# TensorE's program for an expert with further passes: one interleaved stretch instead of a detour and back

## The chip, the cores and the metric

One core of one Trainium2 chip. The metric is the device time of one execution in microseconds (us).

## The reference, cut to what matters

A two-layer encoder over 256 tokens of 1024 channels, all float32. Each layer has a mixing part (three groups of heads side by side between two projections) and an expert part. The change touches the second alone:

```python
g_sel = argmax(g_logits)                      # one of 4 groups per token
top_p, top_i = top_k(softmax(e_logits of that group), 2)
weights = one_hot(expert_id, 32) * combine    # two experts per token
hg, hu = t @ w_gate[e], t @ w_up[e]           # 1024 -> 512, for each of 32 experts
out += (silu(hg) * hu * weights[:, e]) @ w_down[e]   # 512 -> 1024
```

Every expert has 6.3 MB of weights (gate, up and down of 2 MB each), and all 32 of each layer are read from HBM.

## The kernel before, in words

**Passes.** The kernel computes an expert only for tokens that chose it, 32 at a time (`SLOTS`). Each expert has one pass of its own; if more than 32 tokens chose it, further passes ("extra") come before the own one. How many is counted on the chip and read into registers (`extra_passes`, L422, and `passes_before`, L418). A pass is, on TensorE (PE):

- `gather` (L587): 8 matmuls pick the tokens into bank `b_prep`. Each float32 matmul of this kernel is two in the trace, with two weight loads, so the trace has 16.
- `places` (L595): two transposes put the weighted places into `b_places`.
- `hidden` (L601): 32 matmuls (64 in the trace) with gate and up into `b_gate`. It waits for both chunks to have landed.
- `down` (L627): 16 matmuls (32) into `b_y`.
- `combine` (L643): 8 matmuls (16) add the result to the sums in banks 0 to 3.

Between them, VectorE (DVE) compares ranks and weighs (`prep`, L1195), transposes and scales the tokens (`tokens_ready`, L1211), and, behind ScalarE's (ACT) tanh (`act_tanh`, L974), multiplies and transposes the activation (`activate`, L1200). ACT copies `b_places` (`places_copy`, L983) and `b_y` (`y_copy`, L979). The semaphores come in two sets, `M` for own passes and `V` for further ones; `th`, `actT` and the banks are shared by both, while `PwTx` and `ysbx` are the further passes' own copies.

**Order.** In an expert without a further pass, PE runs hidden, gather for the next expert, combine of the expert before, down, places for the next expert (L906 to L928). The code of the own passes lies one behind the other (`pe_expert_n`), and at its end each tests whether the next expert has further passes (L908). If it has, PE jumps to a block `pe_extra_n` behind all own passes of both layers (L941 to L963). There a loop runs gather, places, hidden, down and combine in that order, once for each further pass, and PE jumps back to `pe_expert_n`. Each such block's loop body is written out for its own expert.

**Weights.** They go through a ring of 11 chunks of 2 MB in SBUF during the expert part (`RING` 8 and `LATE` 3, L71). SyncE (SP) issues the loads in a fixed order, each behind the wait for the chunk that held its slot (`wait_freed`, L466): gate and up are free after the own pass's `hidden` (`M["hidden_mm"]`), down after its `down` (`M["down_mm"]`), L483. The experts 0 and 31 of a layer (`EDGES`) load gate and up in halves.

Of the kernel before, what the change touches and what calls it, by code (L numbers as in the profile page):

```python
# [6 lines left out]
ALU = mybir.AluOpType  # L7
ACT = mybir.ActivationFunctionType
# [50 lines left out]
NE = NG * EPG  # L59
FF = 512  # L60
FC = FF // P
SLOTS = 32
NQ = P // SLOTS
GQ, DQ = FF // NQ, D // NQ
MORE = SEQ // SLOTS - 1
HALF = KC // 2
# [179 lines left out]
def build_encoder(nc, x_in, cols, rows, w_in, w_out, w_router, w_gate, w_up, w_down, final_w, out):  # L246
    with ExitStack() as ctx:
# [117 lines left out]
        Pw = [sb(f"Pw{i}", [P, TT, P], at=q) for i in range(2)]  # L365
# [4 lines left out]
        Pb = [sb(f"Pb{i}", [P, TT, SLOTS], at=m2) for i in range(2)]  # L370


        PwT = [sb(f"PwT{i}", [P, TT, P], at=scratch) for i in range(2)]
        PwTx = sb("PwTx", [P, TT, P], at=scratch)
        xg = [sb(f"xg{i}", [P, KC, SLOTS], at=scratch) for i in range(2)]
        ysb = sb("ysb", [P, DQ], at=scratch)
        ysbx = sb("ysbx", [P, DQ], at=scratch)
# [44 lines left out]
        def extra_passes(eng, e):  # L422
            return eng.value_load(more[0:1, e:e + 1], min_val=0, max_val=MORE)
# [159 lines left out]
        def _(pe):  # L583
# [3 lines left out]
            def gather(S, picks):  # L587

                for t in range(TT):
                    for j in range(NQ):  # L590
                        last = mm(b_prep[j * SLOTS:(j + 1) * SLOTS, 0:DQ], picks[:, t, :], xh[:, t, j * DQ:(j + 1) * DQ],  # L591
                                  start=(t == 0), stop=(t == TT - 1))
                last.then_inc(S["gather_mm"], 1)

            def places(S, weighted):  # L595

                for t in range(TT):
                    last = tr(b_places[:, t * P:(t + 1) * P], weighted[:, t, :], ident[:, :])  # L598
                last.then_inc(S["places_mm"], 1)

            def hidden(S, tokens, li, e):  # L601

                if e in EDGES:
                    for half, part in enumerate(("front", "back")):
                        slot, signal, count = chunk(li, part, e)
                        both = ring[:, slot, :].rearrange("p (h n) -> p h n", h=2)
                        pe.wait_ge(signal, count)
                        for k in range(HALF):
                            for j in range(NQ):
                                o = k * FF + j * GQ  # L610
                                last = mm(b_gate[j * SLOTS:(j + 1) * SLOTS, 0:2 * GQ], tokens[:, half * HALF + k, :],  # L611
                                          both[:, :, o:o + GQ], start=(half + k == 0), stop=(half == 1 and k == HALF - 1))
                        last.then_inc(S["hidden_mm" if half else "front_mm"], 1)
                    return

                (a, a_signal, a_count), (b, b_signal, b_count) = chunk(li, "gate", e), chunk(li, "up", e)
                low, high = min(a, b), max(a, b)
                pe.wait_ge(a_signal, a_count)
                pe.wait_ge(b_signal, b_count)
                for k in range(KC):  # L620
                    for j in range(NQ):
                        o = k * FF + j * GQ
                        last = mm(b_gate[j * SLOTS:(j + 1) * SLOTS, 0:2 * GQ], tokens[:, k, :],  # L623
                                  ring[:, low:high + 1:high - low, o:o + GQ], start=(k == 0), stop=(k == KC - 1))
                last.then_inc(S["hidden_mm"], 1)

            def down(S, li, e):  # L627

                slot, signal, count = chunk(li, "down", e)
                if e == NE - 1:  # L630
                    pe.wait_ge(last_down_half, 16 * (li + 1))
                else:
                    pe.wait_ge(signal, count)
                for c in range(FC):
                    if e == NE - 1 and c == FC // 2:
                        pe.wait_ge(signal, count)
                    for j in range(NQ):
                        o = c * D + j * DQ
                        last = mm(b_y[j * SLOTS:(j + 1) * SLOTS, 0:DQ], actT[:, c * SLOTS:(c + 1) * SLOTS],  # L639
                                  ring[:, slot, o:o + DQ], start=(c == 0), stop=(c == FC - 1))  # L640
                last.then_inc(S["down_mm"], 1)

            def combine(S, places_, y):  # L643

                for t in range(TT):
                    for j in range(NQ):
                        r = slice(j * SLOTS, (j + 1) * SLOTS)
                        last = mm(ps[j][:, t * DQ:(t + 1) * DQ], places_[r, t, :], y[r, :],  # L648
                                  start=False, stop=False, skip_group_check=True)
                last.then_inc(S["combined"], 1)  # L650

            for li in range(DEPTH):
# [253 lines left out]
                for e in range(NE):  # L906
                    n = first + e + 1
                    pe.br_lt(extra_passes(pe, e), 1, on_true=f"pe_expert_{n}", on_false=f"pe_extra_{n}")  # L908
                    left_at[n] = nc.cur_bb
                    nc.switch_bb(f"pe_expert_{n}")  # L910
                    pe.wait_ge(M["xg_ready"], n)
                    hidden(M, xg[e % 2], li, e)
                    if e == 0:
                        pe.wait_ge(M["prep_ready"], 2 * first + 2)
                        places(M, Pw[0])
                    if e + 1 < NE:
                        pe.wait_ge(M["prep_ready"], 2 * n + 1)
                        gather(M, Pb[(e + 1) % 2])
                    if e > 0:
                        pe.wait_ge(M["y_copied"], n - 1)  # L920
                        pe.wait_ge(M["places_copied"], n - 1)
                        combine(M, PwT[(e - 1) % 2], ysb)
                    pe.wait_ge(M["actT_ready"], n)
                    down(M, li, e)
                    if e + 1 < NE:
                        pe.wait_ge(M["prep_ready"], 2 * n + 2)
                        pe.wait_ge(M["places_copied"], n)
                        places(M, Pw[(e + 1) % 2])  # L928
# [12 lines left out]
            for li in range(DEPTH):  # L941
                for e in range(NE):
                    n = li * NE + e + 1
                    nc.switch_bb(f"pe_extra_{n}", parent=left_at[n])
                    more_e = extra_passes(pe, e)
                    prev = passes_before(pe, e)
                    with pe.Fori(0, more_e) as j:
                        i = prev + j + 1
                        pe.wait_ge(V["prep_ready"], 2 * i)
                        gather(V, Pb[(e + 1) % 2])  # L950
                        if n > 1:
                            pe.wait_ge(M["places_copied"], n - 1 if e == 0 else n)
                        places(V, Pw[(e + 1) % 2])
                        pe.wait_ge(V["xg_ready"], i)
                        hidden(V, xg[(e + 1) % 2], li, e)
                        if n > 1:
                            pe.wait_ge(M["y_copied"], n - 1)
                        pe.wait_ge(V["actT_ready"], i)
                        down(V, li, e)
                        pe.wait_ge(V["places_copied"], i)  # L960
                        pe.wait_ge(V["y_copied"], i)
                        combine(V, PwTx, ysbx)
                    pe.br(f"pe_expert_{n}")  # L963
            nc.switch_bb("pe_experts_over", parent=last_at)


# [1 line left out]
        def _(act):  # L968
# [5 lines left out]
            def act_tanh(S, li, e, n):  # L974
                act.wait_ge(S["hidden_mm"], n)
                o = gate_half(li, e)
                A(th[:, :], b_gate[:, o:o + GQ], ACT.Tanh, scale=0.5).then_inc(S["tanh_ready"], 1)  # L977

            def y_copy(S, y, n):  # L979
                act.wait_ge(S["down_mm"], n)  # L980
# [159 lines left out]
        def _(dve):  # L1140
# [59 lines left out]
            def activate(S, li, e, n):  # L1200

                dve.wait_ge(S["tanh_ready"], n)
                o = gate_half(li, e)
                v.scalar_tensor_tensor(th[:, :], th[:, :], 1.0, b_gate[:, o:o + GQ], ALU.add, ALU.mult)  # L1204
                dve.drain()
                v.scalar_tensor_tensor(th[:, :], th[:, :], 0.5, b_gate[:, GQ - o:2 * GQ - o], ALU.mult, ALU.mult)
                dve.drain()
                v.transpose(actT[:, :].rearrange("p (c s) -> p c s", c=FC), th[:, :].rearrange("p (q c) -> p c q", c=FC)  # L1208
                            ).then_inc(S["actT_ready"], 1)
# [382 lines left out]
```

## Time and profile before

| | |
|---|---|
| median of 3 runs | 1186.97 us (1186.21 to 1187.02) |
| the profiled execution | 1185.0 us, of which the span is 1183.3 us |
| matmuls (PE), weight loads (PEld) busy | 923.9 us (78%), 587.3 us (50%) |
| DVE, ACT busy | 354.0 us (30%), 202.8 us (17%) |
| share of the DMA queue for data | 88.0% of 16 engines' span |
| HBM read | 433.20 MB |

The span runs from the first instruction to the last of the profiled execution; what is left to its time lies around it. The busy shares are averages over two mixing parts, in which the transfers mostly wait for slots, and two expert parts (about 150 to 590 us and 740 to 1170 us), in which most weights are read. "Issue" in a chain of waits is time in which an engine waited for nothing that the profile shows. A line number is that of the kernel before.

### The profile page before, as it was taken

Reading aid. Unit: us, or ns where it says so; the run is one execution under the profiler, and the core shown is the slowest. Engines: PE = TensorE matmul, PEld = TensorE weight load, DVE = VectorE, ACT = ScalarE, POOL = GpSimd, SP = SyncE. Lnnn points to the kernel's source line nnn. Section 1 sums busy time; section 2 is a strip of 40 time slices with the busy share of each in tenths; the row PEclk is TensorE's granted clock in tenths of the full one; section 3 lists DMA queues with packets and bytes.
Section 4 is the critical chain, followed back from the end, with each engine's and each line's share of the span. In section 5 each row is a group of like instructions: output and inputs, shape, how many; then the busy total and the mean of one; then the engine's idle time right before and its main releaser. Section 6 shows DMA issues by size and latency. Waiting matters only on the chain.

```text
span 1183.3 us, 26463 instructions
## 1 busy us (share of the span) xinstructions
PE 923.9 (78%) x11004; PEld 587.3 (50%) x11004; DVE 354.0 (30%) x1165; ACT 202.8 (17%) x600; POOL 8.1 (1%) x24
## 2 busy tenths in 40 slices
PE   7999889667678786986699988996666666765954
PEld 6877745333344443553388777453333333433532
DVE  4666343111112232231166645321111111111213
ACT  2275211000001010110124652110000000000001
POOL 2000000000000000000000000000000000000000
PEclk9999989887889998998899999898888888888977
DMA  9853489999999999999996326899999999999995
GB/s 340 319 223 143 151 337 428 429 429 430 429 428 428 429 429 428 412 427 431 405 399 257 124 99 252 353 429 428 430 431 427 431 430 428 431 429 428 428 427 208
DMA packets 50633, 436.17 MB, mean 369 GB/s; under 512 B 9408, under 2 KB 13760, under 8 KB 24640
## 3 DMA queue, kind: packets, MB, share of 16 engines
q1 hardware_dynamic: 50496, 434.26, 88.0%
q8 instruction: 96, 1.57, 0.5%
q14 instruction: 41, 0.34, 0.1%
HBM read 433.20 MB, written 1.05 MB: 367 GB/s over the span
## 4 chain that ended last, share of the span: by engine, by line
PE 46%; DMA 39%; DVE 4%; issue 4%; SPq 2%; DVEq 2%; ACT 1%; ACTq 0%
DMA ring<-in_w_up 38%; PE ps L623 13%; PE ps L711 8%; PE ps L639 5%; PE ps L855 5%; PE ps L648 3%; PE ps L591 3%; PE ps L727 2%; PE ps L611 2%; SPq L462 1%; PE ps L716 1%; DMA ring<-in_w_in 1%; SPq L464 1%; PE ps L824 1%; PE ps L774 1%
## 5 line engine op out<-in xcount | busy, mean ns | idle before, releaser
L623 PE MATMUL ps<-ring,xg 128*32 128x256 f32 x4352 | 314.2, 452 | 173.9 <-DMA ring<-in_w_up 168.6
L623 PEld LDWEIGHTS ps<-ring,xg 128*32 128x32 f32 x4352 | 170.0, 129 | 301.4 <-issue 239.9
L1204 DVE SCALAR_TENSOR_TENSOR th<-th,ps 128x128 f32<-128x128 f32 x72 | 20.7, 287 | 588.1 <-ACT th L977 588.1
L639 PE MATMUL ps<-ring,actT 128*32 128x256 f32 x2304 | 139.2, 382 | 14.1 <-issue 13.2
L977 ACT ACTIVATE th<-ps 128x128 f32<-128x128 f32 x72 | 20.0, 277 | 510.2 <-PE ps L623 474.2
L639 PEld LDWEIGHTS ps<-ring,actT 128*32 128x32 f32 x2304 | 69.0, 109 | 75.3 <-DVE actT L1208 22.6
L591 PE MATMUL ps<-xh,Pb 128*32 128x256 f32 x1152 | 79.5, 394 | 23.4 <-issue 19.4
L711 PE MATMUL ps<-hT,ring 128*128 128x256 f32 x416 | 93.5, 382 | 1.0 <-ACT hT L1014 0.8
L711 PEld LDWEIGHTS ps<-hT,ring 128*128 128x128 f32 x416 | 77.8, 190 | 15.0 <-issue 4.4
L648 PE MATMUL ps<-ysb,PwT 32*128 32x256 f32 x992 | 71.6, 403 | 0.0
L981 ACT ACTIVATE ysb<-ps 128x256 f32<-128x256 f32 x64 | 24.5, 383 | 223.9 <-PE ps L639 223.9
L591 PEld LDWEIGHTS ps<-xh,Pb 128*32 128x32 f32 x1152 | 38.8, 113 | 48.0 <-issue 23.5
L855 PE MATMUL ps<-ring,hT 128*128 128x256 f32 x256 | 59.2, 389 | 2.0 <-DVE hT L1426 2.0
L648 PEld LDWEIGHTS ps<-ysb,PwT 32*128 32x128 f32 x992 | 45.2, 186 | 27.5 <-issue 26.1
L855 PEld LDWEIGHTS ps<-ring,hT 128*128 128x128 f32 x256 | 49.0, 194 | 9.8 <-DVE hT L1426 2.4
L1214 DVE STREAM_TRANSPOSE xg<-ps 128x256 f32<-128x256 f32 x72 | 29.9, 415 | 37.3 <-PE ps L591 37.2
L1076 ACT ACTIVATE pbuf<-pbuf,low 128x256 f32<-128x256 f32 x56 | 28.0, 500 | 30.4 <-DVE low L1387 28.4
L1191 DVE TENSOR_TENSOR Pw<-Pb,W 128x256 f32<-128x256 f32 x72 | 30.6, 425 | 7.0 <-issue 0.5
L1216 DVE TENSOR_TENSOR xg<-xg,fnw 128x256 f32<-128x256 f32 x72 | 30.6, 425 | 5.8 <-issue 0.5
L598 PE MATMUL ps<-ident,Pw 128*128 128x128 f32 x144 | 32.3, 307 | 0.0
L1208 DVE STREAM_TRANSPOSE actT<-th 128x128 f32<-128x128 f32 x72 | 29.3, 407 | 6.2 <-issue 0.9
L598 PEld LDWEIGHTS ps<-ident,Pw 128*128 128x128 f32 x144 | 14.7, 143 | 30.8 <-DVE Pw L1191 16.1
(259 smaller groups left out, 681.5 us busy)
## 6 DMA issues: line engine op xcount, KB each, us to landing
ring<-in_w_down SPq DMA_DIRECT2D x62, 2048.0 KB, 40.4
ring<-in_w_gate SPq DMA_DIRECT2D x60, 2048.0 KB, 45.2
ring<-in_w_up SPq DMA_DIRECT2D x60, 2048.0 KB, 46.9
ring<-in_w_in SPq DMA_DIRECT2D x6, 2048.0 KB, 15.5
ring<-in_w_out SPq DMA_DIRECT2D x4, 2048.0 KB, 18.6
ring<-in_w_gate SPq DMA_DIRECT2D x8, 1024.0 KB, 29.3
ring<-in_w_up SPq DMA_DIRECT2D x8, 1024.0 KB, 31.3
ring<-in_w_in SPq DMA_DIRECT2D x6, 1024.0 KB, 16.0
```

Of the source, the lines that this page charges most:

```text
L591: last = mm(b_prep[j * SLOTS:(j + 1) * SLOTS, 0:DQ], picks[:, t, :], xh[:, t, j * DQ:(j + 1) * DQ], start=(t == 0), stop=(t == TT - 1))
L598: last = tr(b_places[:, t * P:(t + 1) * P], weighted[:, t, :], ident[:, :])
L623: last = mm(b_gate[j * SLOTS:(j + 1) * SLOTS, 0:2 * GQ], tokens[:, k, :], ring[:, low:high + 1:high - low, o:o + GQ], start=(k == 0), stop ...
L639: last = mm(b_y[j * SLOTS:(j + 1) * SLOTS, 0:DQ], actT[:, c * SLOTS:(c + 1) * SLOTS], ring[:, slot, o:o + DQ], start=(c == 0), stop=(c == ...
L648: last = mm(ps[j][:, t * DQ:(t + 1) * DQ], places_[r, t, :], y[r, :], start=False, stop=False, skip_group_check=True)
L711: last = mm(bank[:, 0:SEQ], lhs, hT[:, k, :], start=(k == 0), stop=(k == KC - 1))
L855: last = mm(bank[:, t * DQ:(t + 1) * DQ], mixT[:, c, t * P:(t + 1) * P], w_half[c // OUT_ROWS][:, c % OUT_ROWS, j * DQ:(j + 1) * DQ], star ...
L1076: last = A(pb[:, t, :], pb[:, t, :], ACT.Exp, bias=low[:, u, t:t + 1], scale=-1.0, accum_out=den[:, u, t:t + 1])
L1191: return v.tensor_tensor(weighted[:, :, :].rearrange("p t (j s) -> p t j s", j=NQ), picks[:, :, :].unsqueeze(2).broadcast_to(four), W[:, : ...
L1208: v.transpose(actT[:, :].rearrange("p (c s) -> p c s", c=FC), th[:, :].rearrange("p (q c) -> p c q", c=FC)).then_inc(S["actT_ready"], 1)
L1214: v.transpose(to[:, :, :], b_prep[:, 0:DQ].rearrange("p (q k) -> p k q", k=KC))
L1216: v.tensor_tensor(to[:, :, :], to[:, :, :], fnw[:, :].unsqueeze(2).broadcast_to([P, KC, SLOTS]), ALU.mult).then_inc(S["xg_ready"], 1)
```

## The change

An expert 2 to 30 of a layer that has a further pass gets a block in which the last further pass and the own pass are one stretch. PE first combines the expert before, then runs any further passes but the last in a loop as before, guarded by a test, and then, in this order: gather and places (further), hidden (further), hidden (own), down (further), gather for the next expert, combine (further), down (own), places for the next expert. Its last instruction jumps to the next expert's own block or further-pass block. The own block of that expert isn't run then.

The first product of a further pass goes to the bank `b_places` instead of `b_gate`, and ACT's tanh and DVE's activation read it there. So PE waits for ACT's copy of the places before that product and no longer before the combine. The order on ACT, DVE and SP is unchanged.

```diff
 def hidden(S, tokens, li, e):
+    to = b_places[:, 0:2 * GQ] if S is V else b_gate[:, 0:2 * GQ]
...
-                    last = mm(b_gate[j * SLOTS:(j + 1) * SLOTS, 0:2 * GQ], tokens[:, k, :],
+                    last = mm(to[j * SLOTS:(j + 1) * SLOTS, :], tokens[:, k, :],
...
                     pe.br_lt(extra_passes(pe, e), 1, on_true=f"pe_expert_{n}", on_false=f"pe_extra_{n}")
-                    left_at[n] = nc.cur_bb
-                    nc.switch_bb(f"pe_expert_{n}")
+                    left_at[n] = nc.cur_bb if e < 3 else left_at[n - 1]
+                    nc.switch_bb(f"pe_expert_{n}", parent=left_at[n])
...
                     nc.switch_bb(f"pe_extra_{n}", parent=left_at[n])
                     more_e = extra_passes(pe, e)
                     prev = passes_before(pe, e)
-                    with pe.Fori(0, more_e) as j:
-                        i = prev + j + 1
-                        pe.wait_ge(V["prep_ready"], 2 * i)
-                        gather(V, Pb[(e + 1) % 2])
-                        if n > 1:
-                            pe.wait_ge(M["places_copied"], n - 1 if e == 0 else n)
-                        places(V, Pw[(e + 1) % 2])
-                        pe.wait_ge(V["xg_ready"], i)
-                        hidden(V, xg[(e + 1) % 2], li, e)
-                        if n > 1:
-                            pe.wait_ge(M["y_copied"], n - 1)
-                        pe.wait_ge(V["actT_ready"], i)
-                        down(V, li, e)
-                        pe.wait_ge(V["places_copied"], i)
-                        pe.wait_ge(V["y_copied"], i)
-                        combine(V, PwTx, ysbx)
-                    pe.br(f"pe_expert_{n}")
+                    own = 2 <= e < NE - 1
+                    if own:
+                        pe.wait_ge(M["y_copied"], n - 1)
+                        pe.wait_ge(M["places_copied"], n - 1)
+                        combine(M, PwT[(e - 1) % 2], ysb)
+                    def whole(count):
+                        with pe.Fori(0, count) as j:
...
+                    if own:
+                        with pe.If(more_e > 1):
+                            whole(more_e - 1)
+                    else:
+                        whole(more_e)
+                    if not own:
+                        pe.br(f"pe_expert_{n}")
+                        continue
+
+                    i = prev + more_e
+                    pe.wait_ge(V["prep_ready"], 2 * i)
+                    gather(V, Pb[(e + 1) % 2])
+                    pe.wait_ge(M["places_copied"], n)
+                    places(V, Pw[(e + 1) % 2])
+                    pe.wait_ge(V["places_copied"], i)
+                    pe.wait_ge(V["xg_ready"], i)
+                    hidden(V, xg[(e + 1) % 2], li, e)
+                    pe.wait_ge(M["xg_ready"], n)
+                    hidden(M, xg[e % 2], li, e)
+                    pe.wait_ge(V["actT_ready"], i)
+                    down(V, li, e)
+                    pe.wait_ge(M["prep_ready"], 2 * n + 1)
+                    gather(M, Pb[(e + 1) % 2])
+                    pe.wait_ge(V["y_copied"], i)
+                    combine(V, PwTx, ysbx)
+                    pe.wait_ge(M["actT_ready"], n)
+                    down(M, li, e)
+                    pe.wait_ge(M["prep_ready"], 2 * n + 2)
+                    places(M, Pw[(e + 1) % 2])
+                    pe.br_lt(extra_passes(pe, e + 1), 1, on_true=f"pe_expert_{n + 1}", on_false=f"pe_extra_{n + 1}")
...
-                A(th[:, :], b_gate[:, o:o + GQ], ACT.Tanh, scale=0.5).then_inc(S["tanh_ready"], 1)
+                A(th[:, :], (b_places if S is V else b_gate)[:, o:o + GQ], ACT.Tanh, scale=0.5).then_inc(S["tanh_ready"], 1)
...
-                v.scalar_tensor_tensor(th[:, :], th[:, :], 1.0, b_gate[:, o:o + GQ], ALU.add, ALU.mult)
+                both = b_places[:, 0:2 * GQ] if S is V else b_gate[:, 0:2 * GQ]
+                v.scalar_tensor_tensor(th[:, :], th[:, :], 1.0, both[:, o:o + GQ], ALU.add, ALU.mult)
```

The body of `whole` is the loop body of before with the wait for `V["places_copied"]` moved ahead of `hidden`.

## Rows read from the trace of the kernel before

**Rows 1.** The page: its span, PE, transfer rate by slice, instruction queue.

```profile
span 1183.3 us, 26463 instructions
...
PE 923.9 (78%) x11004; PEld 587.3 (50%) x11004; DVE 354.0 (30%) x1165; ACT 202.8 (17%) x600; POOL 8.1 (1%) x24
...
GB/s 340 319 223 143 151 337 428 429 429 430 429 428 428 429 429 428 412 427 431 405 399 257 124 99 252 353 429 428 430 431 427 431 430 428 431 429 428 428 427 208
...
q8 instruction: 96, 1.57, 0.5%
```

**Rows 2.** The chain in order of time (start, us, what): two landings.

```profile
206.49 48.69 DMA ring<-in_w_up
...
264.50 49.19 DMA ring<-in_w_up
```

**Rows 3.** The same chain: an expert without a further pass.

```profile
441.17 0.86 PE ps L591 x16
442.03 1.08 PE ps L648 x16
443.11 1.86 PE ps L639 x32
444.97 0.37 PE ps L598 x2
```

**Rows 4.** ACT's copies of `b_y`: own ones to 323.5 us, all further ones.

```profile
L981 ACT ACTIVATE ysb<-ps x14: 383/383/384, 167.7 to 322.8; 128x256 f32<-128x256 f32 x14
...
L981 ACT ACTIVATE ysbx<-ps x8: 383/383/384, 340.4 to 1101.7; 128x256 f32<-128x256 f32 x8
```

**Rows 5.** SP's timeline (start, us, what): two loads with none between.

```profile
452.80 0.33 SPq L464 DMA_DIRECT2D ring<-in_w_up  x1
486.49 0.33 SPq L464 DMA_DIRECT2D ring<-in_w_down  x1
```

**Rows 6.** SP's line L464, time from issue to landing.

```profile
DMA to landing us min/median/max: 7.5/39.9/50.9
```

**Rows 7.** Windows (PE, PEld, DVE, ACT, POOL busy, then PEclk, DMA share, GB/s).

```profile
458.00:462.00 4.00, 2.56 (x18) 0.90 (x18) 0.61 (x2) 0.09 (x1) 0.00 (x0) 0.50 1.01 426
482.00:486.00 4.00, 4.00 (x76) 2.41 (x72) 0.00 (x0) 0.00 (x0) 0.00 (x0) 1.00 0.93 397
486.00:490.00 4.00, 4.00 (x72) 2.18 (x64) 2.39 (x7) 0.28 (x1) 0.00 (x0) 1.00 0.86 332
```

**Rows 8.** The chain again: expert 18 with one further pass.

```profile
370.66 3.64 PE ps L623 x64
...
379.16 1.11 PE ps L591 x16
...
381.30 3.66 PE ps L623 x64
384.96 1.60 issue
...
388.55 0.39 ACT ysbx L981
...
389.08 1.15 PE ps L648 x16
390.23 3.63 PE ps L623 x64
```

**Rows 9.** The chain again: stops at and in the further passes.

```profile
323.17 6.37 issue
329.54 1.97 PE ps L591 x16
...
357.76 0.93 issue
...
362.53 0.52 issue
...
453.14 6.17 issue
```

More of the change, by code:

```diff
@@ L610, in hidden @@
                                 o = k * FF + j * GQ
-                                last = mm(b_gate[j * SLOTS:(j + 1) * SLOTS, 0:2 * GQ], tokens[:, half * HALF + k, :],
+                                last = mm(to[j * SLOTS:(j + 1) * SLOTS, :], tokens[:, half * HALF + k, :],
                                           both[:, :, o:o + GQ], start=(half + k == 0), stop=(half == 1 and k == HALF - 1))
@@ L963, in _ @@
-                    pe.br(f"pe_expert_{n}")
+                    own = 2 <= e < NE - 1
[5 more added lines that the diff above has]
+                        with pe.Fori(0, count) as j:
+                            i = prev + j + 1
+                            pe.wait_ge(V["prep_ready"], 2 * i)
+                            gather(V, Pb[(e + 1) % 2])
+                            if n > 1:
+                                pe.wait_ge(M["places_copied"], n - 1 if e == 0 else n)
+                            places(V, Pw[(e + 1) % 2])
+                            pe.wait_ge(V["places_copied"], i)
+                            pe.wait_ge(V["xg_ready"], i)
+                            hidden(V, xg[(e + 1) % 2], li, e)
+                            if n > 1:
+                                pe.wait_ge(M["y_copied"], n - 1)
+                            pe.wait_ge(V["actT_ready"], i)
+                            down(V, li, e)
+                            pe.wait_ge(V["y_copied"], i)
+                            combine(V, PwTx, ysbx)
@@ new lines, in _ @@
+                    if own:
[7 more added lines that the diff above has]
+                    i = prev + more_e
+                    pe.wait_ge(V["prep_ready"], 2 * i)
+                    gather(V, Pb[(e + 1) % 2])
+                    pe.wait_ge(M["places_copied"], n)
@@ new lines, in _ @@
+                    places(V, Pw[(e + 1) % 2])
+                    pe.wait_ge(V["places_copied"], i)
+                    pe.wait_ge(V["xg_ready"], i)
+                    hidden(V, xg[(e + 1) % 2], li, e)
+                    pe.wait_ge(M["xg_ready"], n)
+                    hidden(M, xg[e % 2], li, e)
+                    pe.wait_ge(V["actT_ready"], i)
+                    down(V, li, e)
+                    pe.wait_ge(M["prep_ready"], 2 * n + 1)
+                    gather(M, Pb[(e + 1) % 2])
@@ L964, in _ @@
+                    pe.wait_ge(V["y_copied"], i)
+                    combine(V, PwTx, ysbx)
+                    pe.wait_ge(M["actT_ready"], n)
[3 more added lines that the diff above has]
+                    pe.br_lt(extra_passes(pe, e + 1), 1, on_true=f"pe_expert_{n + 1}", on_false=f"pe_extra_{n + 1}")
             nc.switch_bb("pe_experts_over", parent=last_at)
@@ L1203, in activate @@
                 o = gate_half(li, e)
-                v.scalar_tensor_tensor(th[:, :], th[:, :], 1.0, b_gate[:, o:o + GQ], ALU.add, ALU.mult)
+                both = b_places[:, 0:2 * GQ] if S is V else b_gate[:, 0:2 * GQ]
+                v.scalar_tensor_tensor(th[:, :], th[:, :], 1.0, both[:, o:o + GQ], ALU.add, ALU.mult)
                 dve.drain()
-                v.scalar_tensor_tensor(th[:, :], th[:, :], 0.5, b_gate[:, GQ - o:2 * GQ - o], ALU.mult, ALU.mult)
+                v.scalar_tensor_tensor(th[:, :], th[:, :], 0.5, both[:, GQ - o:2 * GQ - o], ALU.mult, ALU.mult)
                 dve.drain()
```

## The prediction

> **What bounds the kernel now.** I read the page first. PE is busy for 78% of the span, but the transfers run at 427 to 431 GB/s in nearly every slice of both expert phases [rows 1]: from the 7th slice of 29.6 us to the 19th, but for 412 in the 17th, and from the 27th to the 39th. Outside these phases they run at a third or two thirds of that, waiting for slots or for work. The shares of the page's chain don't say which of the two sets the length, so I went to single steps of the chain in order of time. In the expert phase one landing of an `up` chunk ends at 206.49 + 48.69 = 255.18 us and another, four experts later, at 264.50 + 49.19 = 313.69 us [rows 2]: 14.63 us an expert. An expert without a further pass costs PE 3.6 + 0.86 + 1.08 + 1.86 + 0.37 = 7.8 us [rows 3, 8]. So the transfers are the bound of both phases, and PE has slack wherever it isn't more than the depth of the ring behind them.
>
> The further passes are eight, and before the first of them 14 experts of layer 1 have copied their product [rows 4]. The timeline of these copies puts them at experts 15, 17, 18, 19, 20 (one each) and 23 (two) of layer 1, and 27 of layer 2. An expert with one costs PE 390.23 - 370.66 = 19.6 us from own product to own product [rows 8], above the 14.63 us of its transfers. So PE falls behind from 15 to 20, gains 7 us at 21 and again at 22, and falls behind once more at 23.
>
> How near that comes to the bound is read off SP. No load is issued from 452.80 to 486.49 us [rows 5], because the ring of 11 chunks is full until the own pass of expert 23 has read its gate and up. The load issued at 452.80 is the 77th chunk, expert 26's `up`. At 14.63 us an expert it lands at 313.69 + 12 x 14.63 = 489.2 us. The shortest load took 7.5 us to land [rows 6] and a chunk takes a third of 14.63, so a new one needs some 2.6 us to begin: 486.49 + 2.6 = 489.1. The queue is at its end just then, and the window from 486 to 490 shows it, 332 GB/s against 429 [rows 7]: 0.9 us lost there, and with 0.3 of the window before it about 1.2 us. This is the only place in layer 1 where PE's lateness costs transfer time. **Every us by which expert 23's own first product ends later than 486.5 is a us of the kernel; ending earlier gives 1.2 us at most.**
>
> **The change part by part.** *The order.* In an expert with one further pass PE waits 1.60 us between the pass's first product and its second, for ACT and DVE, and from 388.55 to 389.08, 0.53 us, for ACT's copy before it combines [rows 8]. Both are filled: the first by the own pass's first product (3.6 us), the second by the gather for the next expert (0.86). What the own pass then waits for, its activation, starts behind ACT's copy of the further pass's product: some 0.4 and then the same 1.60, 2.0 us, while PE gathers and combines for 0.86 + 1.08 = 1.94: no cost. The wait for the copy of the places is now ahead of the product; places 0.37 and a copy like ACT's other one, 0.4, end before the tokens are ready, 1.03 us after the gather (380.27 to 381.30) [rows 3, 8]: no cost. Combining the expert before comes first now, ahead of DVE's work for the pass. So each such expert is 2.13 us shorter, five of them before expert 23: -10.7 us. For expert 23 the own first product ends earlier by all that lay between the two first products, 390.23 - 384.96 = 5.27 us (the wait, the second product, the second wait, the combine), less the moved combine 1.08: -4.2 us. The same -4.2 holds for the loads that wait for the own product in the others. SP waits for the same counts in the same order; nothing is moved past its queue. ACT reads and DVE reads of the first product move to another bank of the same size: nothing.
>
> *The program.* The page has 96 instruction packets with 1.57 MB [rows 1], 16.4 KB each; PE ran 11004 matmuls and as many weight loads, so a packet holds some 230 to 250 instructions with the waits. A pass has 16 + 2 + 64 + 32 + 16 = 130 matmuls, 260 instructions with their loads, some 270 in all. What a jump costs is seen at single places. Entry into pass 15, far from anything run: 6.37 us before the gather, and at 23, past two passes that are skipped, 6.17 us. At 17, past one skipped pass: 0.93 us [rows 9]. Back to an expert just passed: none (the own product follows the combine at 390.23 without a gap) [rows 8]. And in pass 17, entered within what had been loaded, PE stops for 0.52 us until 363.04, 50 instructions into its product [rows 9]: the next packet came about 4.8 us after the jump, which lies between 357.8 and 358.7. So packets are fetched one ahead, a far jump costs 6.3 less an ordinary 0.9, some 5.5 us, and a jump to the next packet waits out what is left of 4.8 us.
>
> The Trainium skill says the same in "Runtime: NRT & Kernel Launch", section "Instruction fetch mechanics": blocks of 256 instructions, fetched sequentially, and a taken branch out of the window forces a fetch. It gives the window as two blocks (and TensorE's memory as larger). The trace speaks against two, since passes and experts alternate without a stop. By two, the return to expert 16 below would be a far jump as well, 3.2 us more, and the time 1207.
>
> With the change a further-pass block has 16 + 2 x (16 + 2 + 64 + 32) + 16 = 260 matmuls, 520 instructions, and a loop body of 270 that is skipped when there is one pass: about 800. Every block is three times as long, begins with a jump over a loop body, and its expert block is no longer run through. My estimates, in the order of running:
> - Expert 15: entry as now. It combines (1.1 us, with the registers read before it 1.5), then jumps 270 instructions on, into the packet just asked for: 4.8 - 1.5 = 3.3.
> - Expert 16: back in the expert region one block further than before, early in need of the next packet: 2.3.
> - Expert 17: the block lies 800 instructions past what was run, a far jump: 5.5, the jump over the body 3.3, and 2.0 for the packet after.
> - 18, 19, 20 follow each other; only the jump over the body: between 0 and 4.8 by where the packets' edges fall, 2.0 each, 6.0.
> - Expert 21: five expert blocks past the last one run, a far jump: 5.5, and 2.5 for the next packet.
> - Expert 23: entry as now, its body is run; 1.0 for the next packet.
>
> Sum 31.4 us. After the present stops of 6 us the gather took 1.97 where it takes 0.86 warm, the granted clock being 0.50, the lower of its two levels (1.2 GHz), after a stretch of 4 us without a matmul [rows 7, 9]; for two more such stops, somewhat shorter, 2.0. So expert 23's own first product ends at 486.5 + 31.4 + 2.0 - 10.7 - 4.2 = 505.0 us. With 2.6 for the load to begin and 489.2 for the end of the queue, the transfers stand still for 18.4 us where they now lose 1.2: **+17 us**. The bounds of the fetch term: from below only the two far jumps, 11.0, since nothing excludes that the short ones are free. That gives 482.6 us, before the queue ends, and -1.2 us. From above every jump over a body and every wait for a next packet is 4.8 and expert 16 a far jump: eight times 4.8 and three times 5.5, 54.9, which is +41 us; they don't all fall badly at once. Earlier stands, which the same count puts at experts 20 and 21, don't add to this one: the largest counts. In layer 2 the one pass has no neighbours, and a single entry with its stops is what the ring bears at expert 15 today: nothing. More instruction packets, a dozen of 16.4 KB, are 0.5 us at most.
>
> The profiled execution spans 1183.3 us and took 1185.0; the median of the runs is 1186.97. I add to the median: 1187 + 17 = 1204 us.
>
> **The rivals.** *The program's supply is no matter* (more is fetched ahead than I read from five jumps, or the jumps over a body are free). Then PE only gains, the 1.2 us come back, and nothing more can, for the transfers are full elsewhere: 1185.8 us, within the 0.2% (2.4 us) that a measurement of this kernel can tell from no change. It decides as long as all new stops before expert 23's own product stay under 16 us. For it: single far jumps are only two. Against: the far jumps at 15 and 23, and the stop at 363.04, which shows that even inside loaded code the next packet was not there. 0.19.
>
> *PE's time is the kernel's time.* The chain passes through PE from 323 to 498 us. If that bound, 2.13 us for each of eight passes would be 17 us, 1170 us. Against it stands a rate of 428 in these same slices, and a queue that never ran out but once. 0.05.
>
> *The order doesn't fill what it says*, each wait coming back behind the own pass's combine: -10.7 becomes about 0, with the fetches on top 1215 us. For it: each exchange between PE, ACT and DVE still runs, and in 1.94 against 2.0 us one of them is covered by a hair. Against: the others have 3.6 us of products over them. 0.04, out of the forecast's side.
>
> **How the numbers follow.** The forecast, slower through a stand of the transfers at experts 20 to 23, has 0.76 with the third rival's 0.04 in it and lies at 1204 us. Its own range is 1192 to 1214, for fetch terms of some 19 to 41 us. Leaving out the case of no harm would leave out 0.19 and half of the tails, so the range goes down to 1186. Faster by over 0.2%: 0.05, from the second rival. Within: 0.19, from the first. Slower: 0.76.
>
> **What would show it.** Right: no load issued for some 45 to 55 us ending near 505 us, and one or two 29.6 us slices of layer 1 well under 428 GB/s; "issue" gaps of 5 to 6 us at the heads of experts 17 and 21 and of 2 to 5 us behind a combine; the 1.60 us before the second product gone. Wrong: expert 23's own first product ending by 487 us, or gaps under 1 us behind the combines. If the gaps are there and the time is not, the depth of the ring was misjudged. If the waits inside the pass are there, the order doesn't do what I took it to do.

## The result and the profile after

The changed kernel takes 1221.85 us (1218.17 to 1224.42, 4 runs), the kernel before 1186.59 in the same comparison: 1.0297 times as long, 95% interval 1.0269 to 1.0326, or 35 us more. The prediction was slower, 1204 us, in a range from 1186 to 1214. The side and the mechanism held; the loss is twice what was forecast, and above the range.

The page of the changed kernel, the lines that answer to [rows 1]:

```profile
span 1216.4 us, 26436 instructions
...
PE 937.1 (77%) x11004; PEld 597.1 (49%) x11004; DVE 354.5 (29%) x1165; ACT 202.0 (17%) x600; POOL 8.0 (1%) x24
...
GB/s 344 340 174 139 211 330 428 429 430 429 429 426 428 414 285 279 346 291 430 426 404 424 116 182 78 351 428 429 429 429 429 430 430 429 430 429 429 427 427 213
...
q8 instruction: 110, 1.80, 0.5%
```

PE runs the same 11004 matmuls, its busy share even falls, and nothing in the busy column looks like 35 us. The loss stands in the rates: layer 2 (slices 27 to 39) is as full as before, and in layer 1 the slices 15 to 18 (of 30.4 us each) fall to 285, 279, 346 and 291 GB/s. Short of 429 by 144, 150, 83 and 138, they lack 515/429 of a slice, 36.5 us of transfers. There are 14 instruction packets more.

The transfers don't stand still once but four times: the windows of 4 us between 412 and 444, 452 and 464, 472 and 484, and 508 and 528 us lack 9.2, 5.9, 7.1 and 13.8 us at 429 GB/s. Two of them (columns as in [rows 7]):

```profile
432.00:436.00 4.00, 4.00 (x79) 2.34 (x72) 1.08 (x4) 0.28 (x1) 0.00 (x0) 1.00 0.10 37
...
520.00:524.00 4.00, 4.00 (x84) 2.91 (x77) 1.53 (x5) 0.18 (x1) 0.00 (x0) 1.00 0.01 4
```

SP's timeline of the changed kernel, the loads that answer to [rows 5]:

```profile
491.56 0.33 SPq L464 DMA_DIRECT2D ring<-in_w_up  x1
523.35 0.33 SPq L464 DMA_DIRECT2D ring<-in_w_down  x1
```

The product of expert 23's own pass releases a load at 523.35 us where it was 486.49: 36.9 us later. The prediction had 505.0. The pause between the two loads is 31.8 us, no longer than the 33.7 of before: the loads ahead of it are late already, behind the products of experts 19, 20 and 21 (issued at 437.54, 458.13 and 479.97 us), and there lie the first three of the four stands. The chain of the changed kernel, part of it, from expert 17 to expert 21, shows where PE lost them (start, us, what; the lines of `hidden`, `down` and `combine` are now L624, L640 and L649):

```profile
363.31 5.78 issue
369.09 2.09 PE ps L649 x16
371.18 2.52 issue
373.69 1.93 PE ps L591 x16
...
376.04 3.35 issue
380.33 9.02 PE ps L624 x128
...
395.60 1.15 PE ps L649 x16
396.75 4.84 issue
401.59 1.94 PE ps L591 x16
...
404.64 8.81 PE ps L624 x128
...
420.85 4.91 issue
...
444.88 2.44 issue
...
463.97 5.13 issue
...
471.83 2.76 issue
```

Read it in pairs. 5.78 us pass at the head of block 17, the combine runs, and 2.52 more pass behind it, where the jump over the loop body is. At 18, 19 and 20 the head costs nothing (the block follows the one before), and the jump 4.84, 4.91 and 2.44. 463.97 and 471.83 are the head of expert 21 and the next packet. What a reader might pass over are the matmuls behind each stop: a gather of 1.94 us for 0.86 to 1.07, and the two first products 8.81 and 9.02 us for 2 x 3.6.

The trace also tells when each packet of the instruction queue lands, and that names the cause of the stops directly. At 18, PE stops from 396.75 to 401.59 us; one packet lands in that time, at 400.06. At 19 it stops from 420.85 to 425.76, and one lands at 424.17. Of the ten new stops nine end 1.4 to 1.7 us after a packet has landed. The tenth, at the head of block 17, ends 2.9 us after it, and that block begins with reads of registers.

Two windows, each from the first stop at expert 15 to the end of expert 23's own first product (columns as in [rows 7]). The kernel before:

```profile
323.00:486.50 163.50, 126.92 (x2023) 69.34 (x2026) 36.10 (x106) 15.81 (x48) 0.00 (x0) 0.96 1.00 427
```

and the changed one:

```profile
323.00:523.35 200.35, 143.39 (x2016) 80.00 (x2011) 36.70 (x107) 15.10 (x46) 0.00 (x0) 0.83 0.85 356
```

Nearly as many matmuls (2016 for 2023) take 143.4 us where they took 126.9, 16.5 us more, and the mean granted clock is 0.83 for 0.96. In `straight_after` (below), which has the same order and no jumps, 1988 matmuls of this stretch take 124.1 us, so it isn't the order that makes them slow.

### The profile page after: what moved, and what is told of

It reads as the page before. It is cut to its first block, busy times and chain, and to the rows that moved or that the text cites. A ratio compares the mean times of both kernels' runs of the same rounds, so it can differ in the third digit from the quotient of the medians.

```text
span 1216.4 us, 26436 instructions
## 1 busy us (share of the span) xinstructions
PE 937.1 (77%) x11004; PEld 597.1 (49%) x11004; DVE 354.5 (29%) x1165; ACT 202.0 (17%) x600; POOL 8.0 (1%) x24
## 4 chain that ended last, share of the span: by engine, by line
PE 51%; DMA 35%; issue 6%; DVE 3%; SPq 2%; ACT 2%; DVEq 1%; ACTq 0%
DMA ring<-in_w_up 32%; PE ps L624 15%; PE ps L712 8%; PE ps L640 7%; PE ps L856 5%; PE ps L649 4%; PE ps L591 3%; DMA ring<-in_w_down 3%; PE ps L728 2%; PE ps L612 1%; PE ps L717 1%; PE ps L598 1%; SPq L454 1%; PE ps L825 1%; SPq L464 1%
## 5 line engine op out<-in xcount | busy, mean ns | idle before, releaser
L624 PE MATMUL ps<-ring,xg 128*32 128x256 f32 x4352 | 325.3, 463 | 180.6 <-DMA ring<-in_w_up 160.6
L624 PEld LDWEIGHTS ps<-ring,xg 128*32 128x32 f32 x4352 | 178.5, 132 | 311.1 <-issue 255.8
L640 PE MATMUL ps<-ring,actT 128*32 128x256 f32 x2304 | 139.8, 382 | 3.5 <-issue 1.6
L640 PEld LDWEIGHTS ps<-ring,actT 128*32 128x32 f32 x2304 | 69.6, 109 | 63.1 <-DVE actT L1246 23.4
L591 PE MATMUL ps<-xh,Pb 128*32 128x256 f32 x1152 | 83.1, 402 | 20.3 <-issue 19.6
L649 PE MATMUL ps<-ysb,PwT 32*128 32x256 f32 x992 | 74.8, 417 | 26.5 <-issue 25.4
L649 PEld LDWEIGHTS ps<-ysb,PwT 32*128 32x128 f32 x992 | 47.3, 192 | 52.4 <-issue 49.2
L1113 ACT ACTIVATE pbuf<-pbuf,low 128x256 f32<-128x256 f32 x56 | 28.0, 501 | 30.4 <-DVE low L1425 28.5
## 6 DMA issues: line engine op xcount, KB each, us to landing
ring<-in_w_in SPq DMA_DIRECT2D x6, 1024.0 KB, 16.4
```

The costliest lines, as they stand in the source:

```text
L624: last = mm(to[j * SLOTS:(j + 1) * SLOTS, :], tokens[:, k, :], ring[:, low:high + 1:high - low, o:o + GQ], start=(k == 0), stop=(k == KC - 1))
L1113: last = A(pb[:, t, :], pb[:, t, :], ACT.Exp, bias=low[:, u, t:t + 1], scale=-1.0, accum_out=den[:, u, t:t + 1])
```

## The experiments

All were compared with the kernel before on the same chip. The theories are those of the expectations: A, stops for the program's supply and the low clock behind them are the whole loss; B, the stops don't hang on jumps; C, the new order itself costs; D, a stop costs its length wherever it stands; E, a jump over a body costs a fixed time. In the last experiment A is split: A1, a stop makes the matmuls behind it slow whatever its cause; A2, only a stop for the program's supply does.

### Both orders without jumps

TensorE's program gets the numbers of further passes that these inputs have, as constants. So their program holds for these inputs alone; they compute all that the others do.

```diff
+MORE_AT = {(0, 14): 1, (0, 16): 1, (0, 17): 1, (0, 18): 1, (0, 19): 1, (0, 22): 2, (1, 26): 1}
...
-                    pe.br_lt(extra_passes(pe, e), 1, on_true=f"pe_expert_{n}", on_false=f"pe_extra_{n}")
+                    for i in range(passed + 1, passed + MORE_AT.get((li, e), 0) + 1):
...
```

> The order of before with the number of further passes of each expert fixed in TensorE's program for these inputs (one at experts 15, 17 to 20 and at 27 of layer 2, two at 23), so that its program has no jump in the expert parts. Theory A (stops for the program's supply, and the low clock behind them, are the whole loss): no stop of over 1 us named issue between experts 15 and 23; expert 23's own first product ends near 469 us against 486.5, the queue of loads never runs out, and the time is 1185 to 1186 us, within 2 us of before. Theory B (the stops are not bound to jumps but to the load on the queues, or to the size of the program): the two stops of 6.2 to 6.4 us at experts 15 and 23 stay.

> The order of the change, counts fixed in the same way, no jump. Theory A: the order by itself gains on TensorE; expert 23's own first product ends near 462 to 467 us, earlier than in straight_before, a step from own product to own product in experts 18 to 20 takes 17 to 18.5 us against some 19.2, and the time is 1185 to 1186 us, the same as straight_before. Theory C (the order itself costs: two first products one after the other, the shared bank, waits that come back behind the combine): the granted clock falls below 0.95 between 323 and 487 us or the step takes over 20 us, and the time stays at or over 1200 us.

`straight_before` took 1183.52 us for 1186.22, ratio 0.9984 (0.9971 to 0.9996); `straight_after` 1182.48 us, ratio 0.9967 (0.9956 to 0.9979). Between the experts 15 and 23 neither has a stop named issue over 2 us. PE's longer waits there are for weights to land (2.44 and 4.08 us in `straight_before`, 4.69, 1.97 and 4.27 us in `straight_after`): it is early. With these waits expert 23's own first product ends at 478.2 and 468.6 us, later than the 469 and the 462 to 467 that were expected, and the order makes it 9.6 us earlier. PE's timeline in `straight_after`, expert 18 (idle before it in brackets):

```profile
377.75 7.11 PE L627 MATMUL ps<-ring,xg 128*32 128x256 f32 x128 [0.75 <-ACT PwTx L1001]
384.66 1.94 PE L643 MATMUL ps<-ring,actT 128*32 128x256 f32 x32
386.38 1.07 PE L594 MATMUL ps<-xh,Pb 128*32 128x256 f32 x16
387.39 1.15 PE L652 MATMUL ps<-ysbx,PwTx 32*128 32x256 f32 x16
388.46 1.93 PE L643 MATMUL ps<-ring,actT 128*32 128x256 f32 x32
```

The five run without a gap. A step to the next such expert takes 16.4 us (377.75 to 394.17), against 19.0 in `straight_before` (370.26 to 389.22 from own product to own product): the order is worth 2.5 us of PE an expert, as meant. Theories B and C fall. Of those 2.5 us, as was forecast, next to nothing reaches the time: the two medians are 1.0 us apart and the intervals overlap. Both are a little faster than the 1.2 us that the stand at 486 us explains. In the profiled executions expert 32's product is copied 2.0 and 2.1 us earlier, and the mixing part of layer 2 adds some 1.2 us to that. Why is open.

### The old order with a jump over a dead body

```diff
                     prev = passes_before(pe, e)
+                    if 2 <= e < NE - 1:
+                        with pe.If(more_e > MORE - 1):
+                            gather(V, Pb[(e + 1) % 2])
+                            places(V, Pw[(e + 1) % 2])
+                            hidden(V, xg[(e + 1) % 2], li, e)
+                            down(V, li, e)
+                            combine(V, PwTx, ysbx)
```

> Before, with a loop body of 261 instructions that never runs (guarded by a test that is false for these inputs) ahead of each further-pass loop of experts 2 to 30, jumped over at every entry. Nothing that is executed changes but one test. Theory A: new stops of 4.5 us behind the entries of 15 and 23, two of 5.3 us at 17, one of 5.3 at 18, and some 3 us of slow matmuls behind each; expert 23's own first product ends 28 to 36 us later than in before, at 515 to 522, and the time is 1213 to 1222 us. Theory C: within 2 us of before.

1234.53 us for 1186.22, ratio 1.0404 (1.0386 to 1.0421): more than the change itself, with the order and every executed matmul as before. The chain of `dead_body`, its stops over 4 us:

```profile
327.65 10.50 issue
...
371.13 12.75 issue
...
425.50 5.25 issue
...
451.39 5.30 issue
...
469.81 4.23 issue
...
500.37 10.89 issue
```

At 15 and 23 the entry takes 10.50 and 10.89 us where it took 6.37 and 6.17 [rows 9], and two packets land in each, one after the other: one for the head and one for the jump's target. At 17, which the trace of before showed to cost 0.93, it is 12.75, with three packets. Expert 23's own product ends at 539.1 us for 515 to 522 expected, and the time is 12 us above the upper end of theory A: it had a stop of 5.3 us at 18 and none behind it. There is none at 18 (nothing over 1.3 us); 425.50 is the head of expert 19, 451.39 that of expert 20, and 469.81 the return to expert 20's own block, so three stops stand where it had one. Why the packets fell this way isn't shown. The side is A's, the places only in part.

### The loop body moved out of the way

```diff
-                        with pe.If(more_e > 1):
-                            whole(more_e - 1)
+                        pe.br_lt(more_e, 2, on_true=f"pe_last_{n}", on_false=f"pe_others_{n}")
```

The blocks `pe_others_n`, with the loop and a jump back, stand behind all others.

> The change, with the loop for the passes before the last moved behind all blocks of both layers, so that a block has 538 instructions for 805 and an expert with one further pass jumps over nothing. Theory A: the stops behind the combine at 15, 17, 18, 19 and 20 go (2.5, 2.5, 4.8, 4.9 and 2.4 us), those at the heads of 17 and 21 stay, and 23, which has two passes, gets two more of 5 us for the way to its loop and back; expert 23's own first product ends at 501 to 508 us, and the time is 1201 to 1208 us. Theory C: the time stays within 5 us of 1222.

1197.20 us, ratio 1.0097 (1.0066 to 1.0128), some 25 us less than the change and 4 us under the expected 1201 to 1208; expert 23's own product ends at 502.4 us, within 501 to 508. The chain of `loop_away`, its stops over 2 us:

```profile
323.25 6.24 issue
...
331.57 2.04 issue
...
355.17 2.14 issue
...
364.65 6.17 issue
...
438.66 5.37 issue
...
446.77 2.74 issue
...
466.31 6.50 issue
...
474.90 4.60 issue
```

None stands between 365 and 438 us, that is at 18, 19 and 20, whose steps take 16.6 us as in the straight program. The heads of 17 and 21 keep theirs. At 15 a stop of 2.04 us stays where none was expected; it lies inside the combine, while a packet lands. Of two stops forecast at 23 only the way out is there (474.90).

### The same blocks against other packet edges

32 matmuls (128 instructions) behind a false test in expert 1's block, so that all later blocks lie 129 instructions further.

> The change with 129 instructions that never run put ahead of the blocks of experts 2 and on, so that the same blocks lie otherwise against the packets' edges. Theory A (packets of 256 instructions, one fetched ahead, a jump waits for what is left): counting on from where the stops stood in the changed kernel, the stops behind the combine become about 2 at 18, 3 at 19 and 5 us at 20, where they are 4.8, 4.9 and 2.4, the stop of 3.4 us behind the gather of 17 goes, and the time falls by 3 to 9 us, to 1213 to 1219 us. Theory E (a jump over a body costs a fixed 2.5 to 5 us wherever it lies): the same stops and a time within 2 us of 1222.

1211.76 us for 1185.59, ratio 1.0217 (1.0200 to 1.0234): some 10 us less than the change, by a piece of program that never runs. E falls. The chain has 1.27, 2.02 and 2.08 us at 18, 19 and 20 for 4.84, 4.91 and 2.44; only the first lies at the jump, the others inside the first product. The stop of 3.35 us behind the gather of 17 is gone. Two places were forecast wrongly, 5 us at 20 and nothing more at 15, where 5.29 stands, and the time is 1 us below the expected 1213 to 1219; so where the packets' edges lie was known only roughly.

### One part alone, and one place alone

> Before with one part of the change alone: the first product of a further pass goes to the bank of the places, and the wait for ACT's copy of the places stands ahead of that product; order and program else as before. Theory A: expert 23's own first product ends within 1 us of 486.5 and the time is within 1.5 us of before. Theory C (the shared bank makes the loss): 5 us or more slower.

> The change for experts 2 to 30 of layer 2 alone, where only expert 27 has a further pass; layer 1 as before. Theory A (lateness costs only once the ring's loads have all landed): the block of expert 27 shows its stops (6 us at the entry, 2 to 5 us behind the combine, one at the head of expert 28), TensorE is up to 10 us later there, no load is late, and the time is within 2 us of before. Theory D (a stop costs its own length wherever it stands): 5 to 10 us slower.

> The change for expert 23 of layer 1 alone, the one whose own product decides when loads go on; all other blocks as before. It has two further passes, so its loop body is run and not jumped over. Theory A: the interleaved stretch lets the own first product end 2 to 5 us earlier, 482 to 485 us against 486.5, a stop of 5 us stands at the head of expert 24 where it delays nothing, and the time is 0 to 1.5 us below before. Theory C: slower by 2 us or more.

```diff
-                    own = 2 <= e < NE - 1
+                    own = li == 1 and 2 <= e < NE - 1    # layer2_only
+                    own = li == 0 and e == 22            # only_23
```

`bank_only` (the hunks of the change in `hidden`, `act_tanh` and `activate`, and the moved wait): 1186.00 for 1185.59 us, ratio 0.9999 (0.9989 to 1.0008). The bank costs nothing that can be told.

`layer2_only`: 1185.67 us, ratio 1.0003 (0.9987 to 1.0019). The chain shows the block of its expert 27 with a stop at its head, which the kernel before has too (6.64 us at 1084.23), and a new one behind the combine:

```profile
1084.82 6.19 issue
1091.01 2.09 PE ps L649 x16
1093.10 2.22 issue
1095.32 1.93 PE ps L591 x16
```

and no time is lost. But this doesn't decide about D, as it was meant to: the expected stop at the head of expert 28 isn't there, the interleaved order makes up for most of the 2.22 us, and PE reaches expert 28's product at 1112.08 us for 1111.10 in the kernel before. So it is 1.0 us late, less than the interval can tell. What decides is `pause_long` below. That there was room is seen at the end of the chain, whose last `up`, issued at 1123.03, lands 41.11 us later.

`only_23`: 1185.59 us, ratio 1.0001 (0.9991 to 1.0010). SP's timeline:

```profile
454.87 0.33 SPq L464 DMA_DIRECT2D ring<-in_w_up  x1
484.64 0.33 SPq L464 DMA_DIRECT2D ring<-in_w_down  x1
```

The pause between the loads is 29.8 us for 33.7, 3.9 less, as A has it. Of the forecast gain of up to 1.2 us nothing is seen, and the interval leaves room for 1.1 us at most. Four windows say where it went:

```profile
482.00:486.00 4.00, 4.00 (x80) 2.93 (x76) 1.11 (x4) 0.00 (x0) 0.00 (x0) 1.00 1.04 426
486.00:490.00 4.00, 4.00 (x72) 2.17 (x63) 2.27 (x7) 0.55 (x2) 0.00 (x0) 1.00 0.95 393
...
498.00:502.00 4.00, 4.00 (x56) 2.00 (x52) 0.00 (x0) 0.14 (x1) 0.00 (x0) 0.70 0.89 377
502.00:506.00 4.00, 4.00 (x69) 2.08 (x61) 2.39 (x7) 0.47 (x2) 0.00 (x0) 1.00 0.89 328
```

Of the dip at 482 to 490 us, 397 and 332 GB/s [rows 7], 393 is left in one window, and another of the same size stands at 498 to 506: the return to expert 24's own block stops PE for 5.17 us, the loads behind it come later, and the queue runs thin there instead. In this trace the gain was given back one expert on.

### A stop of the same length without any fetch

`straight_after`, with a wait of PE behind the combine of experts 17 to 20 for a row of 18 (9) writes of GpSimd.

```diff
+            for number in (17, 18, 19, 20):
+                pool.wait_ge(M["combined"], number - 1)
+                for turn in range(18):
...
+                    g.memset(idle[:, :], 0.0).then_inc(paused, 1)
...
+                            pe.wait_ge(paused, (e - 15) * 18)
```

> straight_after (no jump) with TensorE made to wait, behind the combine of experts 17 to 20, for a row of 18 writes of GpSimd that start when that combine has ended: a stop of some 4 to 5.5 us that has nothing to do with instructions. Theory A1 (a stop of about 5 us itself makes the matmuls behind it slow, whatever its cause): a step from own product to own product in experts 18 to 20 takes 16.4 us plus the stop plus 2.5 to 3.5 us, the gather takes 1.9 us for 1.07, and the granted clock of the 4 us windows behind each stop shows 0.50. Theory A2 (the slowness belongs to the program's supply, instructions that come in haltingly): 16.4 us plus the stop, within 0.5.

> The same with 9 writes, a stop of some 2 to 3 us. Theory A1 with the clock falling only behind a longer stop: 16.4 us plus the stop plus 0 to 0.5 us, gather 1.07 us, granted clock 1.00 throughout. Theory A1 with a cost in proportion to the stop: 1.3 to 1.8 us on top.

PE's timeline of `pause_long`, expert 19:

```profile
402.42 1.15 PE L660 MATMUL ps<-ysb,PwT 32*128 32x256 f32 x16
408.36 1.93 PE L602 MATMUL ps<-xh,Pb 128*32 128x256 f32 x16 [4.80 <-POOL idle L589]
...
411.42 8.71 PE L635 MATMUL ps<-ring,xg 128*32 128x256 f32 x128 [0.50 <-ACT PwTx L1011]
```

It is the picture of the changed kernel, 1.94 and 8.81 us behind 4.84, with GpSimd named as the cause. The steps from 18 to 20 take 23.6 and 23.7 us: 16.4, the stop of 4.80, and 2.4 to 2.5 us of slower matmuls. The granted clock is 0.50 in the 4 us window from 408 us and 0.66 in the next. With the short stop, expert 19 again:

```profile
402.48 1.07 PE L602 MATMUL ps<-xh,Pb 128*32 128x256 f32 x16 [2.45 <-POOL idle L589]
...
404.67 8.59 PE L635 MATMUL ps<-ring,xg 128*32 128x256 f32 x128 [0.75 <-ACT PwTx L1011]
```

The gather is at full speed and the products aren't: 8.59 for 7.11 us, with a granted clock of 0.57 in the window from 404 us. (At expert 18 the gather is slow too, 1.94 us.) The steps take 20.3 and 20.4 us, 1.5 over 16.4 and 2.45. So these stops cost half to two thirds of their length again, though no packet was waited for: A2 falls, and so does the theory of a clock that falls only behind a longer stop.

Each ran once, 1186.08 and 1186.37 us beside 1184.39 for the kernel before. In `pause_long` the stops and the slower matmuls hold PE for some 29 us in all. Its expert 23's own first product ends 18 us later than in `straight_after`, at 486.9 us, where the kernel before has it, and the time is within 2 us of that kernel's. So theory D falls: up to that point a stop takes nothing like its length from the time. Whether the small gain of `straight_after` is lost again, one run can't tell.

## Why the prediction was right in kind and wrong in size

- **The bound.** "Every us by which expert 23's own first product ends later than 486.5 is a us of the kernel": held. The load behind it went out 15.9, 28.7, 36.9 and 52.6 us later in `loop_away`, `edges_moved`, the change and `dead_body`, and the spans grew by 13.1, 26.9, 33.1 and 49.8 us: the same, less 1.8 to 3.8, which stays unexplained. Of the signs, the stops at the heads of 17 and 21 and behind the combines came as named, and the waits of 1.60 us are gone but for the one in the looped pass of 23. The pause of 45 to 55 us in the loads didn't come: it was 31.8 us, as the loads ahead of it were late too. The prediction said rightly that earlier stands don't add to the last lateness, but took the whole of it for one stand; it came in four pieces.
- **The order.** -10.7 and -4.2 us. In the changed kernel the gain can be read only as what is left over: the new stops and the slower matmuls are 35.3 + 16.5 us, the product is 36.9 later, so 14.9 were gained, as forecast. The other runs give 5 x 2.5 us (the straight programs) and 3.9 (`only_23`), 16.4, which is near it but not the same.
- **The term for the program's supply**, 31.4 us, was 35.3. Place by place, forecast and measured: 15, jump 3.3 and 2.53; 16, 2.3 and 2.01; 17, head 5.5 and 4.9 (5.78 less the 0.93 that it had), jump 3.3 and 2.52, next packet 2.0 and 3.35; 18 to 20, 6.0 and 4.84 + 4.91 + 2.44 = 12.2; 21, 5.5 and 5.13, next packet 2.5 and 2.76; 23, 1.0 and none. The one that was off is the middle group. At 18 and 19 no packet was on its way when PE jumped: the last had landed 4.9 and 5.8 us before, the next lands 3.3 us after the jump, and PE waits the whole 4.8 to 4.9 us. The forecast had 2.0 on the mean.
- **The term that failed is the clock's.** The prediction put it as "for two more such stops, somewhat shorter, 2.0", from the gather alone (1.97 for 0.86 us [rows 9]) and for stops of some 5 us only. (It called the stop ahead of that gather 4 us; it was 6.17.) It measured 16.5 us. Two errors are in it. The first products behind a stop are slower too, which the trace of before had in its `hidden` at 332.54 us, 4.27 us for 3.6. And stops of 2.45 us cost 1.5 us on top, as `pause_short` shows, so all ten counted and not two. With 16.5 for 2.0, and 35.3 for 31.4, the sum of the prediction gives 505.0 + 14.5 + 3.9 = 523.4 us, the measured place. As the gain was read as what is left over, this sum has to close; it shows how the miss divides, 14.5 us to the clock and 3.9 to the packets.
- **The rivals.** "The program's supply is no matter" fell with `dead_body`, "PE's time is the kernel's time" with `straight_after` and `pause_long`, and "the order doesn't fill what it says" with the step of 16.4 us. The range's upper end took the fetches for the only doubt; the clock had no bounds of its own.
- **The return of 1.2 us** was no sure thing either: in the trace of `only_23` it is lost again one expert later. Nor was it a firm upper bound: the straight programs are 2.7 and 3.7 us faster than the kernel before.

Of the rule in the Trainium skill ("Runtime: NRT & Kernel Launch", "Instruction fetch mechanics"), the sequential fetch and the stop at a far branch stand as the runs show them: no stop named issue over 2 us between the experts 15 and 23 of a program without jumps, 4.6 to 6.6 us at each far target. The window of two blocks doesn't: `loop_away` returns to expert 16's block, behind a block of 538 instructions, without a stop at its head, and the 2.14 us stand 49 matmuls further on.

No version here beats the kernel before in general. The straight ones do by 0.2 to 0.3%, for inputs whose counts are known.

## What to carry to other kernels

A rearrangement on an engine with a written-out program changes its code layout, and where that has jumps the layout is part of the cost: count the instructions between a jump and its target, and put code that rarely runs behind everything else and not in the way. Then ask by how much the engine may be late before a queue of transfers runs empty, and price the late one alone. Each stop of 2.4 us or more that was measured here took more than its own length from TensorE, since the granted clock was lower behind it for a while.

## What the runs showed of the hardware

- TensorE resumed 1.4 to 1.7 us after an instruction packet had landed at nine of the ten new stops. A stop in which two packets landed one after the other took 10.5 and 10.9 us (`dead_body`).
- With the DMA queues full, a jump over some 260 instructions right behind a block's head cost TensorE 2.4 to 4.9 us in the changed kernel and 0 to 5.3 us in `edges_moved`; a far target cost 4.6 to 6.6 us. 129 instructions that never run moved the time of the kernel by some 10 us.
- A stop of 2.45 us was followed by 1.5 us of extra matmul time, one of 4.80 us by 2.4 to 2.5 us. Behind the short one the granted clock was 0.57 on the mean of the 4 us from 404 us; behind the long one 0.50 in the 4 us from 408 us and 0.66 in the next. The lower of the two levels (1.2 GHz) is 0.50.
